# Forgetting attention on one core: the causal mask moved from TensorE products into the keys' bias

## The reference

```python
s = einsum('bhqd,bkhd->bhqk', q, k) * HEAD_DIM ** -0.5
s = s + cum[query] - cum[key]                 # running sum of log(sigmoid(forget gate))
s = where(key_position <= query_position, s, -inf)
p = softmax(s); o = p @ v
```

## Time and profile before

| what | value |
|---|---|
| median of 3 runs | 1265.19 us |
| the profiled execution's own time | 1265.25 us |
| its span, first to last instruction | 1263.2 us |
| TensorE busy, share of the span | 1188.1 us, 94% |
| TensorE weight loads | 922.0 us, 73% |
| VectorE busy | 879.0 us, 70% |
| ScalarE busy | 740.7 us, 59% |
| granted TensorE clock, mean | 0.981 |

### The profile page before, as it was taken

How to read it: one execution, slowest core, us unless ns; L and a number is a source line. 1 busy time by engine, 2 the same in 40 slices (tenths; PEclk the granted TensorE clock), 3 DMA queues, 4 the chain that set the end, 5 groups by cost and what they waited for, 6 DMA issues and landing times.

```text
span 1263.2 us, 17917 instructions
## 1 busy us (share of the span) xinstructions
PE 1188.1 (94%) x6175; PEld 922.0 (73%) x6175; DVE 879.0 (70%) x1121; ACT 740.7 (59%) x891; POOL 81.7 (6%) x136
## 2 busy tenths in 40 slices
PE   5999999999999995999889999999999999999975
PEld 3898799789879973788766676667666766667641
DVE  7355535644563554666688988898889888988826
ACT  7443445344444534422457777777777777777724
POOL 0010020111100000011100000000000000000013
PEclk9999999999999997899989999999999999999988
DMA  6354363354521001763399999999999999999928
GB/s 186 78 115 111 93 145 96 73 122 104 128 73 50 13 6 39 262 271 151 146 352 370 381 404 392 391 389 406 390 392 391 406 392 391 393 397 398 377 87 340
DMA packets 86215, 306.31 MB, mean 242 GB/s; under 512 B 14664, under 2 KB 39240, under 8 KB 61600
## 3 DMA queue, kind: packets, MB, share of 16 engines
q1 hardware_dynamic: 67680, 241.83, 50.8%
q0 software_dynamic: 11328, 38.80, 11.3%
q10 hardware_dynamic: 7168, 25.17, 5.9%
HBM read 254.36 MB, written 51.41 MB: 242 GB/s over the span
## 4 chain that ended last, share of the span: by engine, by line
PE 55%; DMA 1%; DVE 1%; POOL 1%; issue 1%; ACT 1%; POOLq 0%; ACTq 0%; DVEq 0%
PE banks L129 17%; PE banks L130 17%; PE banks L131 16%; PE banks L1619 2%; PE bank L1213 1%; POOL e_y L1707 1%; PE bank L1662 1%; DMA e_y<-yrows,slot_of 1%; PE banks L1188 1%; PE e_ph L1762 0%; PE banks L1647 0%; DMA raw<-in_w_out_dram 0%; DMA yrows<-m_ys 0%; ACT e_res L1728 0%; ACT m_ys L1442 0%
## 5 line engine op out<-in xcount | busy, mean ns | idle before, releaser
L1570 DVE TENSOR_TENSOR ring_l<-raw,ring_h 128x2048 fp32r<-128x2048 f32 x192 | 436.3, 2287 | 66.5 <-ACT ring_h L1432 63.9
L1432 ACT ACTIVATE ring_h<-raw 128x2048 fp32r<-128x2048 f32 x192 | 367.8, 1918 | 123.9 <-PE banks L131 123.9
L129 PE MATMUL banks<-ring_h,m_xh 128*96 128x512 f32 x512 | 206.9, 404 | 6.4 <-DVE m_xl L1574 4.4
L131 PE MATMUL banks<-ring_h,m_xl 128*96 128x512 f32 x512 | 202.8, 396 | 0.0
L130 PE MATMUL banks<-ring_l,m_xh 128*96 128x512 f32 x512 | 202.7, 396 | 0.0
L129 PEld LDWEIGHTS banks<-ring_h,m_xh 128*96 128x96 f32 x512 | 83.3, 163 | 52.4 <-issue 15.5
L143 PE MATMUL a_pj<-zl,a_wh 128*128 128x348 f32 (+1 forms) x416 | 109.9, 354 | 0.0
L131 PEld LDWEIGHTS banks<-ring_h,m_xl 128*96 128x96 f32 x512 | 83.2, 162 | 36.3
L143 PE MATMUL a_pj<-zh,a_wh 128*128 128x348 f32 (+1 forms) x416 | 109.3, 353 | 0.0
L143 PE MATMUL a_pj<-zh,a_wl 128*128 128x348 f32 (+1 forms) x416 | 108.4, 351 | 0.0
L130 PEld LDWEIGHTS banks<-ring_l,m_xh 128*96 128x96 f32 x512 | 83.4, 163 | 32.1
(11 more groups left out here) (251 smaller groups left out, 1882.2 us busy)
## 6 DMA issues: line engine op xcount, KB each, us to landing
raw<-in_w_gate_dram SPq DMA_DIRECT2D x64, 1024.0 KB, 12.0
raw<-in_w_up_dram SPq DMA_DIRECT2D x64, 1024.0 KB, 10.5
raw<-in_w_down_dram SPq DMA_DIRECT2D x64, 1024.0 KB, 11.3
xrows<-a_kl POOLq DMA_DIRECT2D x51, 256.0 KB, 4.9
a_raw<-in_w_in_dram SPq DMA_DIRECT2D x24, 512.0 KB, 4.1
m_xg<-xrows ACTq DMA_DIRECT2D x32, 384.0 KB, 8.1
yrows<-m_ys ACTq DMA_DIRECT2D x32, 384.0 KB, 7.0
yrows<-a_kl POOLq DMA_DIRECT2D x33, 256.0 KB, 4.9
```

The source lines that it names most:

```text
L129: nc.tensor.matmul(out, xh, wh, start=first, stop=False)
L131: return nc.tensor.matmul(out, xl, wh, start=False, stop=last)
L1432: nc.scalar.activation(wh[s][:], raw[j][:], ACT.Copy).then_inc(S["w_hi"], 1)
L1570: nc.vector.tensor_tensor(wl[s][:], raw[j][:], wh[s][:].bitcast(F32), ALU.subtract).then_inc(S["w_lo"], 1)
```

## The change

The mask leaves TensorE. In steps 0 and 8 VectorE adds the mask of every tile's own keys to the bias tile (1024 columns, the triangle repeated eight times) before the reduction. After step `s` the 128 columns of its tile must be plain bias again for the later, wider steps: ScalarE issues a DMA for them behind the exponential, in steps 0 to 6 and 8 to 14 (56 transfers of 128 x 128 f32 = 64 KB in all). The reduction of every step but 0 and 8 waits for these (`bias_back`). The fp32r copies of identity and mask, made by two ScalarE instructions at the start, go.

```diff
 # buffers and start
-        ident_r = c.sb(ctx, "a_ident_r", [P, P], F32R)
-        mask_r = c.sb(ctx, "a_mask_r", [P, P], F32R)
-                nc.scalar.activation(ident_r[:], c.ident[:], ACT.Copy).then_inc(S["masks_made"], 1)
-                nc.scalar.activation(mask_r[:], c.maskneg[:], ACT.Copy).then_inc(S["masks_made"], 1)
-                pe.wait_ge(S["masks_made"], 2)
 # ScalarE, softmax(s), behind the exponential
+                        if s % NT < NT - 1:
+                            own = slice(w - P, w)
+                            act.dma_start(cb[:, own], c.negcum[bass.ds(i * 2 + s // NT, 1), own].partition_broadcast(P).rearrange(
+                                "p o l -> p (o l)")).then_inc(S["bias_back"], 16)
 # VectorE, ahead of the reduction of step s
                             dve.wait_ge(S["scored"], i * STEPS + (s + 1))
                             if s % NT == 0:
                                 dve.wait_ge(S["cb_in"], i * 32 + (16 * h + 16))
+                                own = cb[:, META:L].rearrange("p (t k) -> p t k", k=P)
+                                mask = c.maskneg[:].rearrange("p (o k) -> p o k", o=1).to_broadcast([P, NT, P])
+                                link(nc.vector.tensor_tensor(own, own, mask, ALU.add))
+                            else:
+                                dve.wait_ge(S["bias_back"], i * (32 * (NT - 1)) + 16 * (s - h))
 # TensorE, scores(s)
-                        a = max(at, w - P)
-                        if a < at + n:
-                            mm = nc.tensor.matmul(ps[:, a:at + n], ident_r[:], mask_r[:, a - (w - P):at + n - (w - P)],
-                                                  start=False, stop=True, skip_group_check=True)
```

More of the change, by code:

```diff
@@ L229, in mixers @@
                  "rden_done", "spread", "meta_kept", "o_scaled", "squared", "averaged", "rooted", "mixed", "cb_in", "taps_in",
-                 "x_copied", "u_done", "gated", "c_squared", "c_averaged", "c_rooted", "c_ln", "o_ln", "masks_made", "blanks_made", "v_chunks", "own", "passed")
+                 "x_copied", "u_done", "gated", "c_squared", "c_averaged", "c_rooted", "c_ln", "o_ln", "bias_back", "blanks_made", "v_chunks", "own", "passed")
         S = {n: c.sem("a_" + n) for n in names}
@@ L688, in _ @@
                 with dve.Fori(0, PAIRS - 1) as i:
-                    chain.enter(i, STEPS + 5)
+                    chain.enter(i, STEPS + 7)
                     pair(i, False)
```

## The result

The changed kernel takes 1319.68 us (median of 4 runs, 1317.9 to 1321.53) against 1264.94 us for the kernel before: a ratio of 1.0432, with a 95% interval of 1.0419 to 1.0445. It is 54.7 us slower. The direction was forecast, the size was not: 1276.5 us, in a range of 1268 to 1289.

The account below looks back on a forecast made before the run. TensorE's program order was taken to set the pace most of the time. Rounds 1 to 3 at +3.1 us each, round 4 +2.1 and the start -0.2 made +11.2 us: 1276.5 us, range 1268 to 1289.

Parts of the forecast that it names:

- The fetch's price: Bias-column fetch in each step: lands 2.1 us after issue, so 2.30 us from `topped` to the next reduction.
- The rate: Steps 1 to 4: each us of extra fetch delay adds some 4.2 us a round.
- just in time: Steps 9 to 15: fetches arrive without delaying the reductions, and 0.66 us from removed mask products is kept.
- the company of other DMAs: GpSimd's bursts on the same DMA engines delay fetches: 0.5 us a round in rounds 1 to 3, between 0 and 2.
- The additions: VectorE's mask addition before the reductions of steps 0 and 8: 1.28 us each, 0.75 in round 4's step 8; 9.7 us.
- The products: 80 mask products on TensorE: removal returns start distances, 6.1 us in four rounds, not full durations, 17.8 us.
- no room at step 1 and at step 8: TensorE's step 1 scores and step 8's next group have no slack to hide the addition: +1.18 and +1.28 us.
- the rival of a fetch behind the exponential's end: Fetch waits for the exponential's end, or is slower by 0.6 to 0.9 us from crowding: 1289 us; chance 0.14.
- The chain of steps 1 to 4: Each reduction waits for its fetch, delaying TensorE: +2.27 us at step 4, +1.99 us kept after steps 5 to 7.
- A fetch always in time: Rival: steps 1 to 4 cost nothing beyond the addition; +3.8 us, 1269 us; chance 0.12.
- nothing to be measured: Rival: additions of 0.7 us with fetches nearly in time, 1265 to 1267 us; chance 0.04.
- The faster side: Rival: each mask product holds TensorE for its whole 0.223 us row, so removal gives 1257 us; chance 0.05.

Follow-up runs that it names:

- e13: Changed kernel with GpSimd's zero-writes in three blocks, each let go near the end of an attention phase and meant to be over before the next: 1299.33 us.
- e15: Changed kernel with fetches from 128 different rows of x (wrong bias values) and the zero-writes in three blocks clear of the attention: 1278.06 us.
- the runs with x: Changed kernel with fetches reading x at a fixed address instead of negcum: 128 rows 1291.5 us, one row 1312.78 us, 128 rows with bursts clear 1278.06 us.
- e7: Changed kernel whose fetches read 128 different rows of x instead of one row of negcum 128 times, bursts left in place: 1291.5 us, single run.
- e9: Changed kernel with fetches from 128 different rows of x and the zero-writes let go at seven places between attention phases: 1287.05 us.
- products off: Kernel before without its 80 mask products on TensorE, everything else the same: 1260.31 us, ratio 0.9963.

## Why the prediction was wrong

**The fetch's price is the step that failed.** "A 64 KB load lands 2.1 us after its issue" was true of its row, a load to 16 partitions from separate rows, and not of this fetch, in which 128 partitions read the same 512 bytes: 2.8 to 2.9 us. From `topped` to the next reduction the prediction took 2.3 us; with the bursts clear it is 3.2 us (`e13`), with separate rows 2.2 us (`e15`). I compared size and overlooked the source. With the bursts clear, that difference is 1299.3 - 1278.1 = 21.2 us, or 22.5 us at the stage's end. A little of it is the computed address, which the runs with x do not have: in the loop the fetch goes out 0.17 us behind `topped` with it, 0.04 us without. The rate was in the prediction, 4.2 us a round for each us of delay: 1 us in four rounds makes 17 us. Steps 1 to 4 kept to it: from the reduction of step 0 to that of step 4, round 2 of `e13` takes 15.9 us and that of `e15` 11.7. What the rate left out are the later steps. The prediction has the fetches of steps 9 to 15 "just in time"; with the shared source steps 10 and 11 take 6.14 and 3.94 us against 5.19 and 3.42, the first because its fetch goes out 2.3 us late as well.

**The second failed term is the company of other DMAs.** I put 0.5 us a round on it, "between 0 and 2", and it cost 20.4 us beside the shared source: clear of the bursts the three rounds are 9.1, 6.5 and 4.5 us shorter. I had priced one fetch as late by tenths. A 64 KB fetch beside the 256 KB writes took up to 6.4 us to its reduction, worst in steps 6 and 11. The half clock behind idle stretches, which the prediction did not have at all, lies mostly in this share: five of its seven places went with the bursts. It does not come from the bursts alone: `e7` has the same bursts and no such place, `e9` has two.

**What held.** The additions: 9.7 us summed, 9.6 us measured. The products: distances and not durations; of the 6.1 us 4.5 came back in the kernel before, 5.8 by the stage's end. The two additions' places, no room at step 1 and at step 8, are in the trace: TensorE stood for 1.12 us ahead of the scores of step 1, and for 0.74 us ahead of its next group in step 8, waiting for the low part. The fetch is issued while the exponential runs, so the rival of a fetch behind the exponential's end is excluded; that it could be "as slow by 0.6 to 0.9 us from crowding" had the right size for the latency and the wrong reason. The chain of steps 1 to 4: with both causes taken away the stage lost 10.4 us against 9.7 us summed. So at a fetch of 1.9 us the form of the sum was right, and two of its prices were not.

**The rivals.** A fetch always in time is excluded by 73.1 us of waits, nothing to be measured by additions of 1.23 us and the same waits. The faster side is excluded by products off, -4.5 us, for it would have needed 0.12 us a product. The Trainium skill's rule (Perfetto Trace Analysis, Identifying the Most-Contended Engine), read as a price, gave 15.1 us; the removal returned 4.5 us, so here the duration of a weight load was not what a product taken out gives back.

**The accounting.** From 1264.9 us: products -4.5, additions +9.6, the loop of a 1.9 us fetch and what does not add up +8.1 (the remainder to 1278.1), shared source with its computed address +21.2, bursts with half clock +20.4: 1319.7 us. The last two depend on the order in which they are taken out: by the single run of `e7`, the separate rows first are worth 28.2 us and the bursts after them 13.4.

## What to carry to other kernels

Before a DMA is put into a step-by-step loop, write down the loop it closes (here maximum, fetch, next maximum) and compare its length with each step, the shortest first; a fetch that is 1 us late in four short steps cost 4 us a round here, whatever its size. Take its price from a row with the same source pattern and the same traffic beside it, not of the same size alone. A copy of 0.22 us from a second on-chip tile, put where the engine idles, did the same work and turned a loss of 55 us into no loss, and, with VectorE's rounds written out, into a gain of 4.

## What the runs showed of the hardware

128 partitions that read the same 512 bytes of DRAM: 2.8 us from issue to landing, against 1.9 us from 128 different rows, same tensor and queue; with 64 bytes a partition still 2.5 us. Beside bursts of 256 KB writes from GpSimd the shared fetch took up to 6.2 us, the one from separate rows up to 5.4. Behind idle time of TensorE inside its busy stage, as that from 234 to 236 us, the granted clock fell to 1.2 GHz for a short stretch, at seven places in the changed kernel's profile and none in that of the kernel before. And with a longer loop body VectorE stood still for 4.9 us at two loop ends, where it waits for 0.45 us in the kernel before; that the length is the cause is argued.
